# Products of two constants at ten stage boundaries of an fp32 two-block transformer kernel

## The chip, the core and the metric

The kernel runs on one core of a Trainium2 chip. A core has a matrix engine (TensorE, PE in the rows), a vector engine (VectorE, DVE), an activation engine (ScalarE, ACT), a general engine (GpSimd, POOL) and a queue that issues transfers (SyncE, SP). The engines run their own instruction streams and wait for each other on semaphores. The metric is device time in microseconds (us) of one execution, the median of several runs.

TensorE's clock has two levels, 2.4 GHz and 1.2 GHz. The trace records the granted clock as a share: 1.00 is 2.4 GHz, 0.50 is 1.2 GHz.

## What is computed

Two transformer blocks of two layers each, in fp32, over 256 tokens of width 1024. Cut to what matters here:

```python
def first_block(x, ...):
    for l in range(2):
        x = x + 0.5 * swiglu(rms_norm(x, ffn1_norm[l]), ffn1_w_gu[l], ffn1_w_down[l])
        x = x + hybrid_mixer(rms_norm(x, mix_norm[l]), w_in[l], ..., w_out[l])
        x = x + 0.5 * swiglu(rms_norm(x, ffn2_norm[l]), ffn2_w_gu[l], ffn2_w_down[l])
    return rms_norm(x, final_norm)

def second_block(x, ...):
    for l in range(2):
        h = hybrid_mixer_2(rmsnorm(x, pre_mix_norm[l]), ...)
        x = x + rmsnorm(h, post_mix_norm[l])
        h = conv_glu_ffn(rmsnorm(x, pre_ffn_norm[l]), ffn_up[l], ..., ffn_down[l])
        x = x + rmsnorm(h, post_ffn_norm[l])
    return x

def rms_norm(x, g):          # rmsnorm is the same
    return x * rsqrt(mean(x * x, -1) + 1e-6) * g
```

## The kernel before

Activations lie transposed: a tile holds 128 channels on the partitions and the 256 tokens along the free axis, so `x` is eight such chunks. All weights stream from HBM once, in slots of 1 MB (`raw`, two buffers). ScalarE rounds a slot to `w_hi`, VectorE computes the rest `w_lo` (L1517), and the ring of split slots is four deep. Activations are split in the same way (`xn`, `h`, `m`, `y`, `yb`, `ya`). Each fp32 product of the model is three products of the split parts, L514 to L516 in `mac`, and L519 to L521 in `mac_tok`, with 128x256 moving operands. `wide` computes two output tiles of 128 channels from a slot; `tokens` computes the transposed form; `down` contracts over the 22 chunks of `h`.

Block 1 runs, per layer, the stages `gu1`, `down1`, `in` (20 slots, attention and a gated spatial unit between them), `pb`, `pa`, `out`, `gu2`, `down2`. Block 2 runs, per layer, `qkv`, `side`, `out`, `gu`, `down`. Each engine has its own program with the stages in this order, and a hardware loop over the two layers of a block, so TensorE's program jumps back once in each block. Nothing schedules it but the order of the code and the semaphores.

A norm needs the sum of squares over all channels. ScalarE squares the eight chunks of `x` as they come out of the stage before, GpSimd adds them into `ssum` (L2049), and `mean_square` lets TensorE multiply `ssum` by the constant `ones_d`, which leaves the mean in every partition of PSUM bank 6 (`AUX`). ScalarE takes the root (`rms`, L1093) and VectorE the reciprocal (`rstd`, L1523). In block 1 the gains alone are applied before the next stage's products, and `rstd` is applied to their results. So those products need only the last chunks of `xn`, and `mean_square` runs between the first two output tiles of the stage. In block 2 some norms can't be put off: after `out`, `mean_square` (k = 1) is followed by `mean_square_direct`, which sums the squares `sq` of the new `x` in eight products (L535), and only then can `xn` be formed. After `down`, `mean_square` (k = 3) is followed by the norm, the addition to `x`, the squares of the next norm and the new `xn`. After block 1 the final norm is applied in the same way (`END1`).

The products in plain fp32 (L529, L535, L822 and others) are not split. `small_product` multiplies all of `xn` by a narrow matrix (`sm_hi` and `sm_lo`, 72 columns, in block 1's `in` after slot 1). `heads4` (L822) issues four products of 128x128 by 128x128.

Of the kernel before, what the change touches and what calls it, by code (L numbers as in the profile page):

```python
# [32 lines left out]
P = 128  # L33
# [104 lines left out]
def cycle(eng, count, period, body):  # L138

    groups = count // period  # L140
    if groups > 1:
        with eng.Fori(0, groups) as g:
            for j in range(period):
                body(j, g)
    else:
        groups = 0
    for j in range(groups * period, count):
        body(j, 0)


def layers(eng):
    return eng.Fori(0, DEPTH)


def program(nc, io, ctx):
# [6 lines left out]
    def fixed(name, shape):  # L162
        t = at_byte(name, shape, cursor[0])
        cursor[0] += (int(np.prod(shape)) * 4 + 31) // 32 * 32
        return t
# [11 lines left out]
    ones_d = fixed("ones_d", [P])  # L177
# [118 lines left out]
    ps = ctx.enter_context(nc.psum_tensor("ps", [P, 8, 512], F32))  # L296
    SC, AUX = 4, 6
# [153 lines left out]
    def run_of(at, k):  # L451

        return k - 1 if at[0] == 2 and k >= 2 else k
# [55 lines left out]
    def _(pe):  # L509
# [8 lines left out]
        def mac_tok(out, xh, xl, w, wl, first, last):  # L518
            pe.matmul(out, xh, w, start=first, stop=False)  # L519
            pe.matmul(out, xh, wl, start=False, stop=False)  # L520
            return pe.matmul(out, xl, w, start=False, stop=last)  # L521

        def mean_square(at, k, by_token=False):
            pe.wait_ge(summed.sem, summed.upto(at, 7 * run_of(at, k)))
            if by_token:
                for t in range(NT):
                    pe.matmul(ps[:, AUX, T + t:T + t + 1], ssum[:, t * P:(t + 1) * P], ones_d[:, 0:1],
                              start=True, stop=True)
            pe.matmul(ps[:, AUX, 0:T], ones_d[:], ssum[:], start=True, stop=True).then_inc(mean_sq.sem, 1)  # L529

        def mean_square_direct(at):

            for c in range(KC):
                pe.wait_ge(squared.sem, squared.upto(at, KC + c + 1))
                last = pe.matmul(ps[:, AUX, 0:T], ones_d[:], sq8[:, c], start=c == 0, stop=c == KC - 1)  # L535
            last.then_inc(mean_sq.sem, 1)

        def xn_ready(at, k, c):

            s = xn_lo_even if c % 2 == 0 else xn_lo_odd  # L540
            pe.wait_ge(s.sem, s.upto(at, k * KC // 2 + c // 2 + 1))

        def gate_up(at, st, k, prev):

            wide(at, st, 0, 0, xn, KC, k - 1, lambda: mean_square(at, k), prev)
            wide(at, st, 1, 0, xn, KC, None, None, prev)
            with pe.Fori(0, (FC - 2) // 4) as g:
                for j in range(2, 6):
                    wide(at, st, j, g, xn, KC)

        def slot(at, st, j, g=0):
            pe.wait_ge(lo.sem, lo.upto(at, st.slot0 + j + 4 * g + 1))
            r = (st.slot0 + j) % RING
            return w_hi[:, r], w_lo[:, r]

        def pair(at, st, i):

            if not isinstance(i, int) or i >= 2 or st.name != "in":
                pe.wait_ge(signals[st.free].sem, signals[st.free].upto(at, st.free0 + (i - 1) * st.free_by))
# [5 lines left out]
        def after(at, behind, q):  # L565

            signal, count, by = behind
            pe.wait_ge(signal.sem, signal.upto(at, count - by * (1 - q)))

        def behind(st):  # L570
            return signals[st.free], st.free0 + st.pairs * st.free_by, st.free_by

        def wide(at, st, j, g, x_of, chunks, k_norm=None, between=None, prev=None):

            whs, wls = slot(at, st, j, g)
            tiles = SLOT // P // chunks
            wh = whs.rearrange("p (c n) -> p c n", c=chunks)
            wl = wls.rearrange("p (c n) -> p c n", c=chunks)
            for f in range(tiles):
                q = (tiles // 2) * j + f // 2  # L580
                if f % 2 == 0 and prev is not None:
                    after(at, prev, q)
                elif f % 2 == 0:
                    pair(at, st, q + 4 * g)
                out = ps[:, 2 * (q % 2) + f % 2, 0:T]
                for c in range(chunks):
                    if k_norm is not None and f == 0 and j == 0:
                        xn_ready(at, k_norm, c)
                    last = mac(out, wh[:, c, f * P:(f + 1) * P], wl[:, c, f * P:(f + 1) * P],
                               x_of[:, c, 0], x_of[:, c, 1], c == 0, c == chunks - 1)  # L590
                last.then_inc(full.sem if f < tiles - 1 else used.sem, 1)
                if between and f == 0:
                    between()

        def down(at, st, hk):
            def tile(j, g):
                pair(at, st, j + 2 * g)
                out = ps[:, 2 * (j % 2), 0:T]
                for half in range(2):
                    pe.wait_ge(lo.sem, lo.upto(at, st.slot0 + 2 * j + half + 4 * g + 1))  # L600
                    pe.wait_ge(h_lo.sem, h_lo.upto(at, hk + (half + 1) * FC // 2))
                    r = (st.slot0 + 2 * j + half) % RING
                    wh = w_hi[:, r, 0:SLOT_DOWN].rearrange("p (c n) -> p c n", n=P)
                    wl = w_lo[:, r, 0:SLOT_DOWN].rearrange("p (c n) -> p c n", n=P)
                    for c in range(FC // 2):
                        k = half * FC // 2 + c
                        last = mac(out, wh[:, c], wl[:, c], h[:, k, 0], h[:, k, 1], k == 0, k == FC - 1)
                    last.then_inc(used.sem, 1)
            cycle(pe, st.pairs, 2, tile)
# [122 lines left out]
        with layers(pe) as layer:  # L732
            at = (1, layer)
            gate_up(at, st1["gu1"], 0, (x_new, 0, 1))
            stage_open(at, st1["gu1"])
            down(at, st1["down1"], 0)

            pe.wait_ge(ready.sem, 16 * N_TABLES)
            for k in range(20):
# [64 lines left out]
            pe.wait_ge(m_lo.sem, m_lo.upto(at, KC))  # L804
            for j in range(4):
                wide(at, st1["out"], j, 0, m, KC)
            gate_up(at, st1["gu2"], 2, behind(st1["out"]))
            stage_open(at, st1["gu2"])
            down(at, st1["down2"], FC)
        mean_square(END1, 0)  # L810
        with layers(pe) as layer:
            at = (2, layer)
            sq, ss, so = st2["qkv"], st2["side"], st2["out"]
# [196 lines left out]
            for b in range(2):  # L1010
                pe.matmul(ps[:, AUX + b, :], ones_q[:], q_diag[:, 2 * b:2 * b + 2].rearrange("p h q -> p (h q)"),
                          start=True, stop=False)
# [9 lines left out]
            pe.wait_ge(yb_lo.sem, yb_lo.upto(at, 2))  # L1022
            for j in range(4):
                wide(at, so, j, 0, y2, KC)
            mean_square(at, 1)
            mean_square_direct(at)
            cycle(pe, FC, 4, lambda j, g: wide(at, st2["gu"], j, g, xn, KC, 1))
            stage_open(at, st2["gu"])
            down(at, st2["down"], 0)
            mean_square(at, 3)  # L1030

    def slot_done(eng, at, st, j, g=0):

        eng.wait_ge(used.sem, used.upto(at, st.slot0 + j + 4 * g + 1))
# [1278 lines left out]
```

## Time and profile before

| | us |
|---|---|
| median of 3 runs | 2209.1 |
| lowest and highest run | 2204.98, 2214.56 |
| profiled execution, first to last instruction | 2211.2 |
| TensorE busy in it | 1995.0 (90%) |
| VectorE, ScalarE, GpSimd busy | 1243.9, 999.5, 703.1 |
| mean granted clock of TensorE | 0.945 |

The profiled execution's own time is its span of 2211.2 us. It lies 2.1 us above the median of the three runs and inside their range. A busy share says which engine is busiest; it doesn't say what an idle stretch waits for. That stands in the timeline, in brackets behind the instruction that ended the idle time: how long the engine sat, and whose result came last. "issue" in that place means that the engine waited for nothing that the profile shows.

### The profile page before, as it was taken

To read this page: it belongs to the slowest core of one execution; us is meant where nothing else is said; L and a number is where in the kernel's file an instruction comes from. 1 tells how busy PE (TensorE), PEld (TensorE's weight loads), DVE (VectorE), ACT (ScalarE), POOL (GpSimd) and SP (SyncE) were. 2 spreads that over 40 slices of the span, in tenths; PEclk is the share of its full clock that TensorE was granted. 3 is DMA by queue.
4 is the path that set the end of the run, shared out by engine and by line. 5 is a ranking of instruction groups with operands and counts; after the bars stand their busy time and mean duration, and the time that the engine had idled before them with its cause. 6 is when DMAs were issued, how large, how long until landed. Compare 5 with 4: busy or idle time off the path is not lost.

```text
span 2211.2 us, 42383 instructions
## 1 busy us (share of the span) xinstructions
PE 1995.0 (90%) x15702; PEld 1947.0 (88%) x15702; DVE 1243.9 (56%) x1541; ACT 999.5 (45%) x1323; POOL 703.1 (32%) x650
## 2 busy tenths in 40 slices
PE   5999988999999999888999888978999689869996
PEld 5999988999999999888999888967989689769996
DVE  4545575665456454765654565526664664356655
ACT  4434444544344344444443455444544363445443
POOL 3661211256317611211564123312331105122221
PEclk8999999999999998999999979988999789989998
DMA  5545433355455454333554522202445322124443
GB/s 184 190 149 192 160 115 134 136 188 190 150 181 202 153 174 173 115 134 119 186 190 148 186 85 96 96 27 107 171 153 170 115 96 96 39 77 152 162 159 135
DMA packets 52105, 314.37 MB, mean 142 GB/s; under 512 B 6928, under 2 KB 9744, under 8 KB 22928
## 3 DMA queue, kind: packets, MB, share of 16 engines
q1 hardware_dynamic: 48960, 311.09, 40.3%
q10 hardware_dynamic: 3024, 1.69, 0.3%
q8 instruction: 74, 1.21, 0.2%
q14 instruction: 47, 0.39, 0.1%
HBM read 311.70 MB, written 1.05 MB: 141 GB/s over the span
## 4 chain that ended last, share of the span: by engine, by line
PE 60%; issue 23%; DVE 5%; POOL 4%; ACT 4%; ACTq 1%; DMA 1%; DVEq 1%; SPq 0%; POOLq 0%
PE ps L514 18%; PE ps L515 18%; PE ps L516 18%; ACT w_hi L1067 2%; PE ps L519 1%; PE ps L521 1%; PE ps L520 1%; DVE conv L1835 1%; ACT conv L1111 1%; POOL lev_c L2149 1%; DMA raw<-in_in_dram 1%; POOL rope_tmp L2093 1%; POOL m L2130 1%; DVE v L2005 1%; DVE w_lo L1517 1%
## 5 line engine op out<-in xcount | busy, mean ns | idle before, releaser
L1517 DVE TENSOR_TENSOR w_lo<-raw,w_hi 128x2048 fp32r<-128x2048 f32 (+1 forms) x322 | 704.9, 2190 | 422.5 <-ACT w_hi L1067 420.8
L514 PE MATMUL ps<-xn,w_hi 128*128 128x256 f32 x2688 | 785.3, 292 | 74.3 <-DVE xn L1538 40.0
L515 PE MATMUL ps<-xn,w_hi 128*128 128x256 f32 x2688 | 773.8, 288 | 0.0
L516 PE MATMUL ps<-xn,w_lo 128*128 128x256 f32 x2688 | 772.9, 288 | 0.0
L1067 ACT ACTIVATE w_hi<-raw 128x2048 fp32r<-128x2048 f32 (+1 forms) x322 | 561.7, 1745 | 103.7 <-DMA raw<-in_down_dram 57.4
L514 PEld LDWEIGHTS ps<-xn,w_hi 128*128 128x128 f32 x2688 | 529.6, 197 | 87.2 <-DVE xn L1538 42.7
L515 PEld LDWEIGHTS ps<-xn,w_hi 128*128 128x128 f32 x2688 | 530.1, 197 | 0.6 <-issue 0.5
L516 PEld LDWEIGHTS ps<-xn,w_lo 128*128 128x128 f32 x2688 | 529.4, 197 | 0.0
L514 PE MATMUL ps<-h,w_hi 128*128 128x256 f32 x1056 | 301.2, 285 | 10.3 <-DVE conv L1835 5.6
L515 PE MATMUL ps<-h,w_hi 128*128 128x256 f32 x1056 | 300.0, 284 | 0.0
L516 PE MATMUL ps<-h,w_lo 128*128 128x256 f32 x1056 | 299.9, 284 | 0.0
L514 PEld LDWEIGHTS ps<-h,w_hi 128*128 128x128 f32 x1056 | 204.0, 193 | 11.6 <-issue 11.5
L2078 POOL TENSOR_TENSOR hv<-hv,rstd 128x256 f32<-128x256 f32 x88 | 156.3, 1776 | 169.9 <-DVE hv L1548 169.9
L515 PEld LDWEIGHTS ps<-h,w_hi 128*128 128x128 f32 x1056 | 204.1, 193 | 0.0
L516 PEld LDWEIGHTS ps<-h,w_lo 128*128 128x128 f32 x1056 | 204.0, 193 | 0.0
L2049 POOL TENSOR_TENSOR ssum<-ssum,sqb 128x256 f32<-128x256 f32 x98 | 91.3, 932 | 276.8 <-ACT sqb L1132 199.2
L1117 ACT ACTIVATE silu_gate<-silu_gate 128x256 f32<-128x256 f32 x88 | 36.8, 418 | 287.0 <-DVE silu_gate L1543 287.0
L2083 POOL TENSOR_TENSOR h<-hv,h 128x256 f32 (+1 forms) x132 | 157.8, 1196 | 23.5 <-POOL h L2081 22.5
L519 PE MATMUL ps<-w_hi,xn 128*128 128x256 f32 x512 | 152.2, 297 | 13.1 <-DVE w_lo L1517 13.1
L520 PE MATMUL ps<-w_lo,xn 128*128 128x256 f32 x512 | 148.1, 289 | 0.0
L521 PE MATMUL ps<-w_hi,xn 128*128 128x256 f32 x512 | 148.0, 289 | 0.0
L1548 DVE TENSOR_TENSOR hv<-silu_gate,ps 128x256 f32<-128x256 f32 x88 | 37.1, 421 | 153.4 <-PE ps L516 134.1
(300 smaller groups left out, 2724.3 us busy)
## 6 DMA issues: line engine op xcount, KB each, us to landing
raw<-in_gu_dram SPq DMA_DIRECT2D x132, 1024.0 KB, 4.7
raw<-in_in_dram SPq DMA_DIRECT2D x70, 1024.0 KB, 4.8
raw<-in_down_dram SPq DMA_DIRECT2D x96, 704.0 KB, 4.0
raw<-in_out_dram SPq DMA_DIRECT2D x16, 1024.0 KB, 4.9
raw<-in_pb_dram SPq DMA_DIRECT2D x4, 1024.0 KB, 4.8
raw<-in_pa_dram SPq DMA_DIRECT2D x4, 1024.0 KB, 4.9
rows<-in_rows_dram SPq DMA_DIRECT2D x2, 768.0 KB, 6.6
x<-in_x_dram SPq DMA_DIRECT2D x1, 1024.0 KB, 4.9
```

The source lines that it names most:

```text
L514: pe.matmul(out, w, xh, start=first, stop=False)
L515: pe.matmul(out, w, xl, start=False, stop=False)
L516: return pe.matmul(out, wl, xh, start=False, stop=last)
L519: pe.matmul(out, xh, w, start=first, stop=False)
L520: pe.matmul(out, xh, wl, start=False, stop=False)
L521: return pe.matmul(out, xl, w, start=False, stop=last)
L1067: return act.activation(out, src, ACT.Copy)
L1517: dve.tensor_tensor(w_lo[:, r, 0:elems], raw[:, k % RAW_RING, 0:elems], w_hi[:, r, 0:elems], ALU.subtract).then_inc(lo.sem, 1)
L1548: dve.tensor_tensor(hv[:, j % 2], silu_gate[:, j % 2], ps[:, 2 * (j % 2) + 1, 0:T], ALU.mult)\
L2049: pool.tensor_tensor(ssum[:], ssum[:], sqb[:, c % 2], ALU.add).then_inc(summed.sem, 1)
L2078: pool.tensor_tensor(hv[:, j % 2], hv[:, j % 2], rstd[:, 0:T], ALU.mult).then_inc(h_scaled.sem, 1)
L2083: pool.tensor_tensor(h[:, i, 1], hv[:, j % 2], h[:, i, 0], ALU.subtract).then_inc(h_lo.sem, 1)
```

## The change

A helper `idle_products(n)` issues `n` plain fp32 products of the constant 128x128 tile `ones_d` with itself into columns 384 to 511 of PSUM bank 7 (`AUX + 1`). Nothing reads them there, and they wait for nothing and signal nothing. It is called at these places on TensorE, and in no other engine's program:

| place | products | executed |
|---|---|---|
| block 1, between `down1` and `in` | 10 | in each of 2 layers |
| block 1, between `out` and `gu2` | 8 | in each of 2 layers |
| block 1, after `down2` (end of the layer loop's body) | 10 | in each of 2 layers |
| after `mean_square(END1, 0)` | 44 | once |
| block 2, between `out` and `mean_square` (k = 1) | 6 | in each of 2 layers |
| block 2, between it and `mean_square_direct` | 16 | in each of 2 layers |
| block 2, between that and `gu` | 16 | in each of 2 layers |
| block 2, between `down` and `mean_square` (k = 3) | 8 | in each of 2 layers |
| block 2, after it (end of the layer loop's body) | 56 | in each of 2 layers |

```diff
--- before.py
+++ after.py
@@ -520,6 +520,11 @@
             pe.matmul(out, xh, wl, start=False, stop=False)
             return pe.matmul(out, xl, w, start=False, stop=last)
 
+        def idle_products(n):
+
+            for _ in range(n):
+                pe.matmul(ps[:, AUX + 1, 3 * P:4 * P], ones_d[:], ones_d[:], start=True, stop=True)
+
         def mean_square(at, k, by_token=False):
             pe.wait_ge(summed.sem, summed.upto(at, 7 * run_of(at, k)))
             if by_token:
@@ -734,6 +739,7 @@
             gate_up(at, st1["gu1"], 0, (x_new, 0, 1))
             stage_open(at, st1["gu1"])
             down(at, st1["down1"], 0)
+            idle_products(10)
 
             pe.wait_ge(ready.sem, 16 * N_TABLES)
             for k in range(20):
@@ -804,10 +810,13 @@
             pe.wait_ge(m_lo.sem, m_lo.upto(at, KC))
             for j in range(4):
                 wide(at, st1["out"], j, 0, m, KC)
+            idle_products(8)
             gate_up(at, st1["gu2"], 2, behind(st1["out"]))
             stage_open(at, st1["gu2"])
             down(at, st1["down2"], FC)
+            idle_products(10)
         mean_square(END1, 0)
+        idle_products(44)
         with layers(pe) as layer:
             at = (2, layer)
             sq, ss, so = st2["qkv"], st2["side"], st2["out"]
@@ -1022,12 +1031,17 @@
             pe.wait_ge(yb_lo.sem, yb_lo.upto(at, 2))
             for j in range(4):
                 wide(at, so, j, 0, y2, KC)
+            idle_products(6)
             mean_square(at, 1)
+            idle_products(16)
             mean_square_direct(at)
+            idle_products(16)
             cycle(pe, FC, 4, lambda j, g: wide(at, st2["gu"], j, g, xn, KC, 1))
             stage_open(at, st2["gu"])
             down(at, st2["down"], 0)
+            idle_products(8)
             mean_square(at, 3)
+            idle_products(56)
 
     def slot_done(eng, at, st, j, g=0):
```

TensorE's program between block 2's `out` and the direct mean, before: the last products of `out`, the product of `ssum` (L529), and the first of the eight products of `sq` (L535).

```order
L514 MATMUL ps<-y_143,w_hi 128x256
L515 MATMUL ps<-y_143,w_hi 128x256
L516 MATMUL ps<-y_143,w_lo 128x256
L524 REGISTER_ALU
L529 MATMUL ps<-ssum,ones_d 128x256
L534 REGISTER_ALU
L535 MATMUL ps<-sq_141,ones_d 128x256
```

The same place in the changed kernel, where the lines are numbered 5 higher:

```order
L514 MATMUL ps<-y_143,w_hi 128x256
L515 MATMUL ps<-y_143,w_hi 128x256
L516 MATMUL ps<-y_143,w_lo 128x256
L526 MATMUL ps<-ones_d 128x128 x6
L529 REGISTER_ALU
L534 MATMUL ps<-ssum,ones_d 128x256
L526 MATMUL ps<-ones_d 128x128 x16
L539 REGISTER_ALU
L540 MATMUL ps<-sq_141,ones_d 128x256
```

Six products now stand ahead of the product of `ssum`, and sixteen between it and the first square; nothing has changed places.

TensorE's program at the end of block 1, before: the end of the loop in `down2` (L142), the end of the layer loop (L732) with its jump back to `gu1`, and `mean_square(END1, 0)`.

```order
L516 MATMUL ps<-h,w_lo 128x256
L142 REGISTER_ALU
L142 COMPARE_AND_BRANCH
L732 REGISTER_ALU
L732 COMPARE_AND_BRANCH
L529 MATMUL ps<-ssum,ones_d 128x256
L811 UNCONDITIONAL_BRANCH
```

And in the changed kernel, where the layer loop is L737:

```order
L516 MATMUL ps<-h,w_lo 128x256
L142 REGISTER_ALU
L142 COMPARE_AND_BRANCH
L526 MATMUL ps<-ones_d 128x128 x10
L737 REGISTER_ALU
L737 COMPARE_AND_BRANCH
L534 MATMUL ps<-ssum,ones_d 128x256
L526 MATMUL ps<-ones_d 128x128 x44
```

The ten products stand ahead of the layer loop's jump back, so TensorE's program reaches that jump behind them; the 44 stand ahead of block 2.

## Rows read from the trace of the kernel before

**Rows 1.** Timeline of TensorE, fp32 passes: start us, us, engine, line, operation, count.

```profile
1426.34 2.02 PE L822 MATMUL ps<-t_inv,lev_c 128*128 128x128 f32 x16
...
1442.38 1.27 PE L822 MATMUL ps<-v_new,k_dec 128*128 128x128 f32 x5
```

**Rows 2.** Stretches: length, busy per engine, then PEclk (granted clock), DMA share, GB/s.

```profile
242.40:252.60 10.20, 10.20 (x50) 10.20 (x50) 4.68 (x6) 2.33 (x3) 0.00 (x0) 0.50 0.45 176
...
853.40:870.40 17.00, 15.63 (x73) 15.63 (x74) 9.85 (x11) 3.91 (x6) 0.00 (x0) 0.50 0.34 124
...
1279.00:1283.40 4.40, 4.35 (x20) 4.35 (x21) 2.62 (x3) 1.26 (x5) 3.21 (x4) 0.50 0.01 4
...
1368.00:1437.00 69.00, 68.80 (x582) 66.92 (x581) 35.12 (x39) 28.57 (x43) 29.62 (x20) 1.00 0.26 92
...
1519.00:1525.80 6.80, 6.79 (x28) 6.13 (x28) 3.76 (x8) 4.94 (x8) 2.31 (x3) 0.50 0.01 2
...
1744.90:1751.00 6.10, 6.09 (x29) 6.10 (x29) 2.50 (x3) 1.71 (x7) 3.20 (x4) 0.50 0.01 4
```

**Rows 3.** Timelines, end of `down1` to `in`; brackets hold the idle time and its releaser.

```profile
224.80 0.28 PE L519 MATMUL ps<-w_hi,xn 128*128 128x256 f32 x1
...
235.62 1.92 ACT L1067 ACTIVATE w_hi<-raw 128x2048 fp32r<-128x2048 f32 x1 [0.83 <-DMA raw<-in_in_dram]
...
240.59 0.30 PE L519 MATMUL ps<-sm_hi,xn 128*128 128x72 f32 x1 [2.87 <-DVE sm_lo L1672]
...
854.77 0.43 PE L519 MATMUL ps<-sm_hi,xn 128*128 128x72 f32 x1 [4.33 <-DVE sm_lo L1672]
...
298.61 0.57 PE L519 MATMUL ps<-w_hi,xn 128*128 128x256 f32 x1 [6.53 <-DVE w_lo L1517]
...
915.31 0.57 PE L519 MATMUL ps<-w_hi,xn 128*128 128x256 f32 x1 [6.54 <-DVE w_lo L1517]
```

**Rows 4.** Timeline of TensorE, end of `out` to `gu2`, first layer.

```profile
450.27 0.28 PE L516 MATMUL ps<-m,w_lo 128*128 128x256 f32 x1
...
450.39 0.28 PE L514 MATMUL ps<-xn,w_hi 128*128 128x256 f32 x1
```

**Rows 5.** Timelines, end of `down2`: into the second layer, then into block 2.

```profile
645.43 0.38 PE L514 MATMUL ps<-xn,w_hi 128*128 128x256 f32 x1 [2.03 <-issue]
...
1265.35 0.70 PE L529 MATMUL ps<-ssum,ones_d 128*128 128x256 f32 x2 [2.97 <-POOL ssum L2049]
...
1279.05 0.58 PE L514 MATMUL ps<-xn,w_hi 128*128 128x256 f32 x1 [13.00 <-DVE xn L1538]
```

**Rows 6.** Timelines, end of block 2's `out` to `gu`, first layer.

```profile
1503.42 0.70 PE L529 MATMUL ps<-ssum,ones_d 128*128 128x256 f32 x2 [1.92 <-POOL ssum L2049]
...
1508.40 5.56 PE L535 MATMUL ps<-sq,ones_d 128*128 128x256 f32 x16 [4.28 <-ACT sq L1485]
...
1512.54 2.29 DVE L1517 TENSOR_TENSOR w_lo<-raw,w_hi 128x2048 fp32r<-128x2048 f32 x1
...
1514.74 1.75 DVE L1523 RECIPROCAL rstd<-rms 128x256 f32<-128x256 f32 x1
...
1518.41 0.39 PE L514 MATMUL ps<-xn,w_hi 128*128 128x256 f32 x1 [4.45 <-DVE xn L1538]
...
1523.74 0.58 PE L514 MATMUL ps<-xn,w_hi 128*128 128x256 f32 x1
```

**Rows 7.** Timelines, end of block 2's `down`: first layer, then the kernel's end.

```profile
1726.11 0.70 PE L529 MATMUL ps<-ssum,ones_d 128*128 128x256 f32 x2 [1.93 <-POOL ssum L2049]
...
1744.90 0.58 PE L514 MATMUL ps<-xn,w_hi 128*128 128x256 f32 x1 [18.10 <-DVE xn L1538]
...
2193.79 0.70 PE L529 MATMUL ps<-ssum,ones_d 128*128 128x256 f32 x2 [1.93 <-POOL ssum L2049]
...
2208.84 1.63 DVE L2001 TENSOR_SCALAR v<-x,gains 128x256 f32<-128x256 f32 x2
```

**Rows 8.** A stretch as in rows 2, around the end of `down2` in the first layer.

```profile
643.50:650.00 6.50, 4.57 (x36) 4.52 (x37) 3.01 (x3) 4.40 (x7) 1.43 (x2) 1.00 0.40 159
```

## Prediction

> **What bounds the kernel now.** I read four views: busy shares, TensorE's timeline, granted clock by stretch, and the bracket behind each instruction that ended an idle time. TensorE is busy for 90% of the span, so the span is its work at its pace plus its waits. Whatever is added to it where it doesn't wait is added to the span. In a full stage the products of the split parts start 0.12 us apart [rows 4]. At the lower clock, 50 of them took 10.20 us [rows 2]. So a restart at 1.2 GHz costs about half of the TensorE time that it lasts, where nothing else is late.
>
> For each of the ten places three questions are to be asked: does TensorE wait there, for whom, and at which clock does it go on?
>
> **The price of one product.** Plain fp32 products appear as two passes each: the eight products of `sq` in the code are the 16 records of L535 [rows 6]. Sixteen passes with a 128x128 moving tile took 2.02 us at the full clock. Less the last one's 0.28 us that is 0.116 us from start to start, so 0.23 us per product. At the lower clock five took 1.27 us [rows 1]: less 0.41 us for the last, 0.215 us a pass, 0.43 us a product. I take 0.23 us, since the clock was at 1.00 through 69 us in which many such passes ran [rows 2]. So 6, 8, 10, 16, 44 and 56 products take 1.4, 1.9, 2.3, 3.7, 10.2 and 13.0 us.
>
> The Trainium skill, "TensorE: Matmul & The Clock Gate", section "Back-to-back issue gap", gives N / 2.4 + 2.5 ns between isolated matmuls, which is 56 ns for 128 columns. By it ten products would take 0.6 us and all the terms below would shrink. The trace has twice that for each of two passes.
>
> **`out` to `gu2`, 8 products, twice.** TensorE doesn't wait here: the first product of `gu2` starts 0.12 us after the last of `out` [rows 4], and the clock is full. The products cover nothing, and the mean that the drain of `gu2` needs comes later by as much. Cost 2 x 1.9 = 3.7 us (1.86 each).
>
> **`down1` to `in`, 10 products, twice.** No wait either: the first product of `in` follows without a bracket [rows 3]. But two slots later TensorE waits 2.87 us (4.33 us in the second layer) for `sm_lo`. That comes from VectorE, behind a `w_lo` whose `w_hi` waited for a transfer [rows 3]. The transfer doesn't depend on the added products. So 2.3 us of delay disappears in this wait, at no cost; without that cover it would be 2 x 2.3. In return the wait shrinks by 2.3 us. TensorE now comes out of it at or into the lower clock, for 10.2 and 17.0 us [rows 2]. Part of this is the narrow product itself (72 columns), which stays. I expect the fall about 2.3 us later, so that 2.3 us more of the work runs at full pace: 1.1 us per layer, -2.2 in all. The bounds are 0 and half of both stretches' busy time, (10.2 + 15.6) / 2 = 12.9. That it reaches the end I read from the next long wait: it is 6.53 us in one layer and 6.54 in the other [rows 3], although the stretches ahead differ by 7 us, so that chain moves with TensorE.
>
> **After `down2`, 10 products, twice.** In the first layer the wait is 2.03 us and its releaser is "issue" [rows 5]: not data, and at the same stage end elsewhere (`down1`) TensorE didn't wait at all. What differs is the layer loop's jump back. Ten products ahead of the jump move it, and the 2.03 us come again behind them. So +2.3 us. If the 2.03 us were a wait for data it would be +0.1. The clock is full before and after [rows 8], so nothing comes back. In the second layer no jump is taken; TensorE waits 2.97 us for `ssum` [rows 5] and 2.3 fit: 0.
>
> **44 products after the final norm's mean.** 10.2 us in a wait of 13.00 us [rows 5]: they end some 2.8 us before `xn` comes. After 2.87 us of waiting the clock also fell at 240.59 [rows 2, 3]. I take 0; the bound is half of 4.35 us, -2.2 [rows 2].
>
> **Block 2, `out` to `gu`, 6 + 16 + 16, twice.** 1.4 us in 1.92, 3.7 in 4.28, 3.7 in 4.45 us [rows 6]: all covered, with under 1 us left each time. So the clock should stay full here. The eight products of `sq` then end earlier, but `rstd` starts at 1514.74 when the 2.29 us of `w_lo` on VectorE are over [rows 6]: that gain is 0. In the first tile of `gu` the chunks of `xn` come one by one; the eighth starts at 1523.74 [rows 6], and only from there to 1525.8, where the clock was full again [rows 2], does pace count. 2.1 us at half pace are 1.0 at full, less what the first pass still waits: -0.9 us per layer, -1.8 in all. Bounds: 0 and -3.4 each.
>
> **Block 2, `down` to the next layer, 8 + 56, twice.** 1.9 us in 1.93 [rows 7] doesn't delay the mean. 13.0 us in 18.10 leave 5 us idle before 1744.90, more than the waits after which the clock fell; the restart stays slow. The jump back, now behind the products, has those 5 us. 0, bound -3.0. At the kernel's end the 56 products stand behind the last mean (2193.79, 0.70 us) and end near 2207.5; VectorE works on `x` until 2210.5 [rows 7]. 0, and 7 us more if they ran at the lower clock.
>
> **Sum.** 3.7 + 2.3 - 2.2 - 1.8 = +2.0 us, on 2211.2 us. The median of the runs is 2.1 us lower, so 2209.1 + 2.0 = 2211.1 us.
>
> **Rivals.**
> - *The clock comes back everywhere.* All restarts run at 2.4 GHz, because it is enough that products ran in most of the wait. The stretches of rows 2 give (10.2 + 15.6 + 4.4 + 6.1) / 2 and twice 6.8 / 2: 24.9 us; less the 6.0 of pure cost that is -18.9, 2190 us. Against it: 2.8 and 5 us idle remain, and the narrow product stays. Half of it is needed to pass 0.5%. Chance 0.08. The Trainium skill, same page, section "What's actually happening", puts the ramp penalty under 1% of a typical span, 22 us here; the stretches' 24.9 us come out just above it.
> - *Nothing comes back.* The clock falls as before, since where it falls depends on where the waits lie. Then only 3.7 + 2.3 = 6.0 us stand: 2215.1 us. For it: each stage meets a changed timing, and falls elsewhere may grow. Chance 0.22.
> - *The jump back is hidden.* If the sequencer gets to the jump well before the products have run, +2.3 becomes +0.1: 2208.9 us. Chance 0.12.
> - *The products run at the lower clock.* That is the slower end, one mechanism: TensorE falls to 1.2 GHz on products that the clock's control doesn't count, and each takes 0.43 us. Then 8 cost 3.4 us twice, the jump's 10 cost 4.3, `down1`'s exceed 2.87 by 1.4, the second 10 their wait by 1.2, 44 (18.9 us) theirs by 5.9, block 2's 6 + 16 + 16 by about 5 per layer, 8 by 1.3 twice, 56 (24.1 us) by 5.8, and at the end by 7. Together 45 us, 2254 us. It decides from 0.27 us per product on (16 of them then fill 4.28 us), and passes 0.5% at about 0.33. Against it: rows 1 and the 1.00 of 1368 to 1437 [rows 2]. Chance 0.08.
>
> **Chances and range.** The forecast has 0.50. Forecast, nothing back and hidden jump together have 0.84, all within 0.5% (11 us, about what a measurement can tell from no change). Faster takes the first rival, 0.08; slower the last, 0.08; the same 0.84. The range takes the three inner cases, the bound of the `down1` term partly, and runs that spread over 10 us: 2202 to 2221.
>
> **What the new profile would show.** Two passes of L526 per product, 0.115 us apart. The first product of `gu2` 1.9 us behind the last of `out`. The wait for `sm_lo` near 0.6 and 2.0 us. At the jump, 2 us of "issue" behind the ten products. Clock 1.00 from the end of block 2's `out` to `gu`, `rstd` still behind `w_lo`. 0.50 at the restarts after 44 and 56. I am wrong if the restarts after 44 and 56 are at 1.00, if passes start over 0.15 us apart, or if the time of a stage between the places has changed by more than 3 us.

## The result, and the profile after

The changed kernel takes 2215.9 us, the median of 20 runs (2209.79 to 2222.04), beside 2208.19 us (2204.63 to 2215.04) for the kernel before in 20 runs on the same chip. The ratio is 1.0030 with a 95% interval of 1.0022 to 1.0038: 6.6 us slower, between 4.9 and 8.4 (the two medians lie 7.7 us apart; all differences below are the ratio's). Forecast were 2.0 us more. That is within the 0.5% that I called "the same", but more than three times the forecast.

First the page of the changed kernel: busy time, share and instructions of each engine, and the granted clock in 40 slices.

```profile
PE 2059.3 (93%) x16310; PEld 2009.6 (91%) x16310; DVE 1243.8 (56%) x1541; ACT 1000.0 (45%) x1323; POOL 701.7 (32%) x650
...
PEclk8999899999999999999999989989999989999999
```

TensorE is busy for 2059.3 us where it was 1995.0. The mean granted clock rose from 0.945 to 0.960, and the span rose too, from 2211.2 to 2215.2 us. So the products do raise the clock, and it buys no time.

**Where time was added.** Timeline of TensorE in the changed kernel, the end of `out` and then the end of `down2` in the first layer of block 1 (answering rows 4 and 5; the number in a bracket is the idle time ahead). The VectorE row is the making of the first weight tile of `gu1`.

```profile
451.30 1.95 PE L526 MATMUL ps<-ones_d 128*128 128x128 f32 x16
453.00 0.36 PE L514 MATMUL ps<-xn,w_hi 128*128 128x256 f32 x1
...
641.53 2.29 DVE L1531 TENSOR_TENSOR w_lo<-raw,w_hi 128x2048 fp32r<-128x2048 f32 x1 [2.15 <-ACT w_hi L1081]
...
645.07 2.39 PE L526 MATMUL ps<-ones_d 128*128 128x128 f32 x20
651.48 0.38 PE L514 MATMUL ps<-xn,w_hi 128*128 128x256 f32 x1 [4.02 <-DVE w_lo L1531]
```

The first is as forecast: 16 passes, and `gu2` starts behind them. The second isn't. Ten products take 2.39 us, but the idle time behind them is 4.02 us where it was 2.03 [rows 5]. From the start of the products to the first product of `gu1` are 6.41 us; before, the same stretch (from 0.12 us after the start of `down2`'s last product, where a next product would start) had 2.2 us. The bracket names `w_lo`, since a later one ended just before; but the first tile of `gu1` was ready at 641.53 + 2.29 = 643.82, 7.7 us before. What TensorE waits for there is what the experiments are about. Right behind it the clock falls, which it didn't before [rows 8]. That fall isn't the jump's alone: four kernels below that have no products at this place (the 10 after `down1` alone, block 2's alone, all but the 10, and the longer fillings) show it too, and in them `gu1` takes 130.0 to 130.1 us from its first product to the first of `down1`, as here; in the kernel before it takes 128.5.

**Where the clock changed.** Stretches of the changed kernel, with the columns of rows 2: `in`, both layers; behind the jump; the restart after the 44 products; block 2's `out` to `gu`; the restart after the 56; and the 44 and the 56 products themselves.

```profile
239.80:253.40 13.60, 12.97 (x61) 12.97 (x62) 6.46 (x7) 3.17 (x6) 0.00 (x0) 0.50 0.43 155
864.40:871.20 6.80, 6.80 (x34) 6.80 (x34) 4.90 (x6) 2.33 (x3) 0.00 (x0) 0.50 0.46 154
652.80:656.20 3.40, 3.40 (x18) 3.31 (x17) 0.00 (x0) 0.00 (x0) 0.00 (x0) 0.50 0.70 282
1280.90:1284.20 3.30, 3.30 (x16) 3.14 (x16) 2.17 (x3) 0.81 (x4) 2.76 (x4) 0.50 0.00 0
1485.70:1660.00 174.30, 166.75 (x1317) 159.20 (x1315) 117.68 (x148) 85.67 (x119) 50.72 (x73) 1.00 0.41 144
1748.50:1751.80 3.30, 2.75 (x13) 2.75 (x14) 2.92 (x4) 2.26 (x9) 2.89 (x4) 0.50 0.02 5
1267.50:1277.30 9.80, 9.80 (x88) 9.61 (x87) 9.43 (x15) 2.98 (x7) 3.57 (x4) 1.00 0.33 109
1730.00:1743.00 13.00, 13.00 (x114) 12.89 (x114) 11.92 (x20) 3.33 (x8) 3.40 (x4) 1.00 0.24 83
```

The last two are long stretches at full clock in which only the added products run. In the kernel before, the clock was at 0.50 in the same two waits (same columns):

```profile
1266.50:1279.00 12.50, 0.00 (x0) 0.00 (x0) 12.01 (x20) 4.68 (x14) 6.41 (x8) 0.50 0.24 84
1727.30:1744.80 17.50, 0.00 (x0) 0.00 (x0) 15.61 (x27) 4.30 (x12) 6.03 (x8) 0.50 0.19 62
```

TensorE's busy time there is 0.00. A low clock on an idle engine costs nothing, and a high one gives nothing back. A third wait of this kind is behind TensorE's last product, at the kernel's end. Most of the rise of the mean is this: by the clock's records the time at 0.50 fell from 247 to 179 us, and the part of it in which TensorE worked on the model's own products from 168 to 154.5 us only.

**The waits that the products fill.** Timeline of the changed kernel: `in`; then into block 2; then block 2's `out` to `gu`; then `down` to the next layer (answering rows 3 and 5 to 7).

```profile
240.43 0.43 PE L519 MATMUL ps<-sm_hi,xn 128*128 128x72 f32 x1 [3.02 <-DVE sm_lo L1686]
...
1267.31 9.99 PE L526 MATMUL ps<-ones_d 128*128 128x128 f32 x88
1280.51 0.38 PE L514 MATMUL ps<-xn,w_hi 128*128 128x256 f32 x1 [3.21 <-DVE xn L1552]
...
1507.57 0.70 PE L534 MATMUL ps<-ssum,ones_d 128*128 128x256 f32 x2 [0.58 <-POOL ssum L2063]
...
1512.55 5.52 PE L540 MATMUL ps<-sq,ones_d 128*128 128x256 f32 x16 [0.71 <-ACT sq L1499]
...
1516.68 2.28 DVE L1531 TENSOR_TENSOR w_lo<-raw,w_hi 128x2048 fp32r<-128x2048 f32 x1
1518.89 1.74 DVE L1537 RECIPROCAL rstd<-rms 128x256 f32<-128x256 f32 x1
...
1522.55 0.39 PE L514 MATMUL ps<-xn,w_hi 128*128 128x256 f32 x1 [0.92 <-DVE xn L1552]
...
1730.46 12.67 PE L526 MATMUL ps<-ones_d 128*128 128x128 f32 x112
1749.05 0.58 PE L514 MATMUL ps<-xn,w_hi 128*128 128x256 f32 x1 [5.92 <-DVE xn L1552]
```

Waits of 13.00, 1.92, 4.28, 4.45 and 18.10 us have become 3.21, 0.58, 0.71, 0.92 and 5.92. Waiting was replaced by products; nothing starts earlier for it. `rstd` still follows `w_lo` on VectorE (1516.68 + 2.28 = 1518.96).

### The profile page after: what moved, and what is told of

It reads as the page before. It is cut to its first block, busy times and chain, and to the rows that moved or that the text cites. A ratio compares the mean times of both kernels' runs of the same rounds, so it can differ in the third digit from the quotient of the medians.

```text
span 2215.2 us, 43599 instructions
## 1 busy us (share of the span) xinstructions
PE 2059.3 (93%) x16310; PEld 2009.6 (91%) x16310; DVE 1243.8 (56%) x1541; ACT 1000.0 (45%) x1323; POOL 701.7 (32%) x650
## 3 DMA queue, kind: packets, MB, share of 16 engines
HBM read 311.70 MB, written 1.05 MB: 141 GB/s over the span
## 4 chain that ended last, share of the span: by engine, by line
PE 60%; issue 24%; POOL 5%; DVE 4%; ACT 4%; ACTq 1%; DMA 1%; DVEq 1%; SPq 0%; POOLq 0%
PE ps L514 18%; PE ps L515 18%; PE ps L516 18%; DVE conv L1849 1%; PE ps L519 1%; PE ps L521 1%; PE ps L520 1%; ACT w_hi L1081 1%; ACT conv L1125 1%; POOL lev_c L2163 1%; DMA raw<-in_in_dram 1%; POOL rope_tmp L2107 1%; POOL m L2144 1%; DVE w_lo L1531 0%; ACTq L1217 0%
## 5 line engine op out<-in xcount | busy, mean ns | idle before, releaser
L514 PE MATMUL ps<-xn,w_hi 128*128 128x256 f32 x2688 | 783.1, 291 | 46.1 <-DVE w_lo L1531 18.9
L2097 POOL TENSOR_TENSOR h<-hv,h 128x256 f32 (+1 forms) x132 | 152.0, 1152 | 23.5 <-POOL h L2095 22.5
```

Of the source, the lines that this page charges most:

```text
L514: pe.matmul(out, w, xh, start=first, stop=False)
L2097: pool.tensor_tensor(h[:, i, 1], hv[:, j % 2], h[:, i, 0], ALU.subtract).then_inc(h_lo.sem, 1)
```

## The experiments

All kernels are the one before with some of the products (the helper `idle_products` is in each). A diff with only + lines is against the kernel before, one with - lines against the changed kernel. Every figure for a kernel is from 12 runs of it (11 for the 10 after `down1` alone and for two products) and 23 or 34 of the kernel before on the same chip. Differences in us are the ratio times some 2209 us. Each timeline is one execution. First the ten places in groups.

**The 10 after `down2` alone.**

```
             down(at, st1["down2"], FC)
+            idle_products(10)
         mean_square(END1, 0)
```

> Only the ten products after down2 of block 1 (run in both layers), nothing else of the change. Theory after the result: nearly the whole loss sits at the layer loop's jump back. The trace of the changed kernel shows 4.02 us of idle behind the ten products where before there were 2.03 us, and the clock falling behind it. So 2.3 (products) + 2.0 (longer idle) + 1.2 (restart at the lower clock) = about 5.5 us slower, ratio 1.0025, with about 4 us of idle behind the products. Rival, the prediction's price: the idle of 2.03 us comes again unchanged and the clock stays full, +2.3 us, ratio 1.001. Second rival: the 4.02 us were chance of one execution; then the idle here is about 2 us.

Measured: 1.0019 (1.0008 to 1.0030), 4.2 us more (1.8 to 6.6). One fifteenth of the products makes more than half of the 6.6 us, by the middle of the intervals. Timeline of this kernel at the jump:

```profile
643.17 2.39 PE L526 MATMUL ps<-ones_d 128*128 128x128 f32 x20
...
649.01 0.57 PE L514 MATMUL ps<-xn,w_hi 128*128 128x256 f32 x1 [3.44 <-issue]
```

Here the bracket says "issue", as in the kernel before: 3.44 us where 2.03 stood.

**All of the change but these 10.**

```
             down(at, st1["down2"], FC)
-            idle_products(10)
```

> The whole change without the ten products after down2. Theory: the jump's place is the loss, so this returns about 5.5 of the measured 6.6 us: within 2 us of the kernel before, ratio 0.9995 to 1.0010, idle at the jump 2.0 us. Rival: the loss is spread over all places (products ahead of gu2, ahead of in, restarts met by other clock falls); then this stays 4 us or more slower, ratio 1.002 or more.

Measured: 0.9993 (0.9980 to 1.0005), -1.5 us (-4.4 to +1.1). Without this call the change is level with the kernel before, although the products of all other places are left, the 8 after `out` too. The mean clock of its trace is 0.959, as in the full change. So most of the time lies at the jump. How much, this pair doesn't fix: taken out of the whole change the 10 give back 8.1 us, alone they cost 4.2, each with about 3 us to either side.

**The 8 after `out` alone.**

```
                 wide(at, st1["out"], j, 0, m, KC)
+            idle_products(8)
             gate_up(at, st1["gu2"], 2, behind(st1["out"]))
```

> Only the eight products between out and gu2, twice. Prediction's price: nothing covers them, 2 x 1.86 = +3.7 us, ratio 1.0017. Rival from the trace of the changed kernel: 0.69 us of each are taken by the wait of 0.24 us for the first drain of gu2 and the late start behind it, so +1.2 each, +2.3 us, ratio 1.0010.

Measured: 1.0016 (1.0001 to 1.0032), 3.5 us (0.2 to 7.1). The trace has `gu2` 1.7 us later at its start, and less behind its first slots, one of which TensorE enters in the kernel before after a wait of 0.24 us for `hv`, and in this one without: at the first product of `down2` 0.9 us are left (130.2 us from the end of `out` instead of 129.3), 1.8 in all for both layers, inside the interval. The kernels with these 8 among others have the same 0.9 in their traces. The kernel without the 10 measured -1.5 (-4.4 to +1.1) with them; with 1.8 us of cost here, its other places would have given back at least 0.7 us. A restart at the full clock in its trace (see the longer fillings) may be a part of that.

**Block 2's products alone** (44, and 6 + 16 + 16 + 8 + 56 in each layer).

```
         mean_square(END1, 0)
+        idle_products(44)
...
+            idle_products(6)
             mean_square(at, 1)
+            idle_products(16)
             mean_square_direct(at)
+            idle_products(16)
...
+            idle_products(8)
             mean_square(at, 3)
+            idle_products(56)
```

> Only the products behind block 1: 44 after the final norm's mean, and 6, 16, 16, 8 and 56 in block 2's layers. Prediction's price: 0 for 44, 8 and 56, and -0.9 us per layer from the first tile of gu, together -1.8 us, ratio 0.9992. Rival A: they give nothing, ratio 1.0000, because the pace of the first tile is set by xn and the clock falls elsewhere. Rival B: they cost, since each layer's stages meet other clock falls, over +1 us. Clock 1.00 from the end of out to the body of gu, 0.50 at the restart behind the 44 and the 56.

Measured: 1.0001 (0.9988 to 1.0014), +0.2 us (-2.7 to +3.1), with the mean granted clock at 0.961 instead of 0.945. This is the cleanest sight of the point above: the clock's mean rises by 0.016, and no change of the time shows.

**The 10 after `down1` alone.**

```
             down(at, st1["down1"], 0)
+            idle_products(10)
```

> Only the ten products between down1 and in, twice. Prediction's price: the 2.3 us vanish in the wait for sm_lo, and the clock falls 2.3 us later: -1.1 each, -2.2 us, ratio 0.9990. Rival: the wait absorbs them and nothing comes back, since the narrow product behind it lets the clock fall anyway: 0, ratio 1.0000. Rival: not absorbed, +4.6 us, ratio 1.0021. The wait for sm_lo itself should be 0.6 to 2.0 us long.

Measured: 0.9998 (0.9985 to 1.0011), -0.4 us (-3.3 to +2.4). The 2.3 us twice are absorbed in the wait for `sm_lo`: without that cover they would cost 4.6 us, which the interval excludes. The clock still falls, in this trace for 3.41 and 10.24 us where it was 10.24 and 17.07. But the second figure is no sign of the products: with none at this place, the trace of the 10 behind the jump (next) has 10.24 us there too. The forecast's -2.2 us is neither shown nor excluded.

**What happens at the jump.** Four explanations were open for the 4 us: (a) the start of a layer's code takes a time of its own after the jump, hidden in part under what is still queued; (b) straight-line code got longer; (c) it doesn't matter where the products stand, and the longer idle time was chance; (d) something that the load of the code collides with. First, the same ten products behind the jump:

```
             at = (1, layer)
+            idle_products(10)
             gate_up(at, st1["gu1"], 0, (x_new, 0, 1))
```

> Ten products at the top of block 1's layer loop, so behind its jump back instead of ahead of it, and nothing else of the change. In layer 0 they run before any data is there and cost nothing. Theory (the products ahead of the jump delay the jump itself, and the refetch behind it takes the same time again): here the idle in front of the products is that of before, 2.0 us, and then 2.3 us of products, +2.3 us at most, less what is waited for anyway; total idle around the jump 2.0 us. Rival (it is only the products' own 2.3 us, wherever they stand, and the longer idle of d2_only was chance): the same time as d2_only, which measured +4.2 us.

Measured: 1.0008 (0.9994 to 1.0022), 1.8 us (-1.3 to +4.8). In the timeline the idle time is ahead of the products and short, and `gu1` follows them at once:

```profile
642.82 2.47 PE L526 MATMUL ps<-ones_d 128*128 128x128 f32 x20 [1.52 <-issue]
645.04 0.36 PE L514 MATMUL ps<-xn,w_hi 128*128 128x256 f32 x1
```

From the end of `down2` to `gu1` are 3.9 us, against 5.8 with the products ahead of the jump and 2.2 with none. Ten products cost 1.7 us here, less than they last, and 3.6 there, so (c) falls by the timelines. The measured times, 1.8 and 4.2, have intervals that overlap and don't tell the two apart by themselves.

**Twice as many ahead of the jump.**

```
             down(at, st1["down2"], FC)
+            idle_products(20)
```

> Twenty products after down2 of block 1 instead of ten, nothing else of the change. Theory (idle behind the products is the fetch after a late jump, 3.4 to 4.0 us at ten): 4.6 us of products and 2 to 4 us idle behind them in layer 0; in the second layer 4.6 us of products in the 3.1 us until ssum is there, +1.5. Sum 4.6 + 0 to 2 + 1.5 = 6 to 8 us slower. If the time until the jump's data arrive counted from the last product of down2, the idle would shrink to about 0 to 1 us and the sum to about 4 us.

Measured: 1.0024 (1.0012 to 1.0036), 5.3 us (2.7 to 8.0), while ten more products last 2.2 us by themselves. The second layer's 20 outlast their wait of 2.97 us, but in the trace `xn` comes no later for it: block 2 starts 16.8 us after the end of `down2`, as in the kernel before. The first product of `gu1` comes 6.6 us after `down2`, against 5.8 with ten:

```profile
641.12 4.62 PE L526 MATMUL ps<-ones_d 128*128 128x128 f32 x40
...
647.72 0.38 PE L514 MATMUL ps<-xn,w_hi 128*128 128x256 f32 x1 [1.98 <-DVE w_lo L1523]
```

So the extra time at the jump is no fixed sum behind the products. With 20 the idle time is 1.98 us again, with 10 it was 3.44.

**The ten products as a loop of five times two**, which makes the code shorter by eight of them and adds jumps of its own:

```
             down(at, st1["down2"], FC)
+            with pe.Fori(0, 5):
+                idle_products(2)
```

> The ten products after down2 of block 1 as a hardware loop of five passes over two products, nothing else of the change: the same 2.3 us of TensorE's time ahead of the layer loop's jump back, but two products of code instead of ten. Theory (ten products of straight code make TensorE load a further piece of its program, and the load behind the jump waits for that one): without that piece the idle behind the products is that of before, 1.5 to 2.1 us, and the total from the last product of down2 to the first of gu1 4.0 to 4.4 us instead of 5.8; about +2.5 us, ratio 1.0011. Rival (the idle is longer because of the products' time ahead of the jump, not their code): 3.4 to 4.0 us idle behind them and +4.2 us, as d2_only.

Measured: 1.0021 (1.0010 to 1.0031), 4.6 us (2.2 to 6.9), with 3.49 us of idle time behind them. Code length, (b), falls: in the traces with 10 and 20 in a row a further piece of the program is loaded 0.4 and 0.6 us before the end of `down2`, in the loop's none, and both with ten wait alike.

```profile
647.24 2.39 PE L526 MATMUL ps<-ones_d 128*128 128x128 f32 x20
...
653.12 0.57 PE L514 MATMUL ps<-xn,w_hi 128*128 128x256 f32 x1 [3.49 <-issue]
```

**Two and six products.** If something collides, the cost should come in a step; if each product adds its share, it should not.

```
             down(at, st1["down2"], FC)
+            idle_products(2)
```

> Two products after down2 of block 1, nothing else of the change. Theory, from all traces so far: behind the layer loop's jump back TensorE loads a 16 KB piece of its program. The load starts 1.0 us behind the jump, but not while a weight transfer of 1 MB is under way: with the jump 1.8 us ahead of the end of down2 it starts before the next transfer (kernel before and six others, first product of gu1 1.9 to 2.3 us behind the end of down2); with ten products the jump comes into the transfer and the load starts when that ends (5.8 to 6.4 us). Two products move the jump by 0.46 us, the load would start 0.4 us ahead of the end of down2, the transfer 0.2 us ahead: still in front. So gu1 starts 2.3 to 2.8 us behind the end of down2, and the time is that of the kernel before, ratio 1.0002. Rival (each product adds its share of what ten cost, 0.38 us): 2.9 us; there the two hardly differ, this run is the lower half of a pair.

Measured: 0.9994 (0.9984 to 1.0004), -1.3 us (-3.5 to +0.9).

```
             down(at, st1["down2"], FC)
+            idle_products(6)
```

> Six products after down2 of block 1, nothing else of the change. Theory as for two: six products move the jump by 1.4 us, so the load would start 0.5 us behind the end of down2, inside the transfer, and waits for its end. So gu1 starts 5.8 to 6.4 us behind the end of down2, as with ten, with 4.4 to 5 us idle behind the products, and the time is that of d2_only: about +4 us, ratio 1.0018. Rival (each product adds its share of what ten cost, 0.38 us): 4.3 to 4.5 us, with 2.9 to 3.1 us idle, +2.3 us. Second rival (products and nothing else): 3.5 us, 2.1 us idle, +1.4 us.

Measured: 1.0019 (1.0009 to 1.0030), 4.2 us (2.0 to 6.6): as much as ten. Two products show no cost, six cost all of it. The timelines of the two kernels, one after the other:

```profile
641.26 0.60 PE L526 MATMUL ps<-ones_d 128*128 128x128 f32 x4
...
643.89 0.38 PE L514 MATMUL ps<-xn,w_hi 128*128 128x256 f32 x1 [2.03 <-issue]
```

```profile
644.91 1.50 PE L526 MATMUL ps<-ones_d 128*128 128x128 f32 x12
...
650.77 0.58 PE L514 MATMUL ps<-xn,w_hi 128*128 128x256 f32 x1 [4.36 <-issue]
```

What differs is in the DMA view, which lists the queues with packets, MB and share of the 16 engines. Kernel before, 641.3 to 643.2 us; the first line is that stretch in 40 slices:

```profile
DMA  0000000000000000000000900000000000009900
...
q1 hardware_dynamic: 7, 0.06, 23.6%
q8 instruction: 1, 0.02, 3.9%
```

The packet of the queue "instruction" at 642.4, 16 KB, I take for a piece of TensorE's program: the view doesn't name the engine, but in the table below it follows TensorE's jump. It comes ahead of the weight transfer (q1), which begins at the right edge. Now the kernel with six products, 644.3 to 648 us, and then 648 to 649:

```profile
DMA  0000096900049509894998999299299699949900
...
q1 hardware_dynamic: 137, 1.05, 79.7%
```

```profile
DMA  9800000000000000000000000000000000000000
...
q8 instruction: 1, 0.02, 6.0%
```

The weight transfer of 1.05 MB has begun first, and the program's piece comes when it is nearly over. `gu1` starts 2.8 us later. The instants, in us from the end of `down2`, taken 0.12 us after its last product starts (the jump is the start of the sequencer's branch instruction in the trace, the piece the start of the first 16 KB packet behind it):

| products ahead of the jump | jump | program's piece | first product of `gu1` | idle behind products | ratio |
|---|---|---|---|---|---|
| none (before) | -1.8 | -0.9 | +2.2 | 2.03 | 1 |
| 2 | -1.6 | -0.1 | +2.6 | 2.03 | 0.9994 |
| 6 | -0.6 | +3.1 | +5.9 | 4.36 | 1.0019 |
| 10 | +0.35 | +3.0 | +5.8 | 3.44 | 1.0019 |
| 10, as a loop | +0.6 | +3.1 | +5.9 | 3.49 | 1.0021 |
| 10, whole change | +0.3 | +3.6 | +6.4 | 4.02 | 1.0030 |
| 20 | +2.6 | +3.6 | +6.6 | 1.98 | 1.0024 |
| 10 behind the jump | -1.8 | -0.8 | +3.9 (products +1.7) | none (1.52 ahead) | 1.0008 |

In all of them `gu1` (or, in the last row, the products) starts 2.5 to 3.1 us after the piece of program. The piece comes 0.9 to 1.4 us after the jump if no weight transfer is in its way, and else up to 0.45 us before the end of the transfer's last packet, some 3 us after `down2`, wherever in the transfer the jump falls. So between 2 and 6 products there is a step of 3.2 us in the start of `gu1`, and then none until the jump itself comes as late as the transfer's end. SP's issue of that transfer isn't moved by the products (642.07 us in the kernel before, 642.01 with ten). (d) stands, and (a) holds as a part of it.

The same order holds elsewhere in the kernel. By the packet records, the trace of the kernel before has 192 single weight transfers of 1.05 MB, some 3.5 us each and 30% of the span. Of its 74 pieces on this queue 20 start inside one of these, all in the last fifth. Over the 14 kept traces 306 pieces start inside such a transfer, 275 of them in the last fifth; if they came at any time alike it would be some 61. The 31 others say that it isn't a strict rule.

What this doesn't show is why the load seldom passes the transfer; it was seen as an order in time only. The transfer wasn't moved or made shorter, which would have been the direct test.

**Longer fillings in block 2.** With block 1's calls gone, I fitted the counts so that less idle time is left at the restarts:

```
         mean_square(END1, 0)
-        idle_products(44)
+        idle_products(54)
...
             mean_square(at, 3)
-            idle_products(56)
+            idle_products(68)
```

> Block 2's products alone, with 54 instead of 44 after the final norm's mean and 68 instead of 56 at the end of the layers, so that under 1 and about 3 us stay idle before the restarts; no products in block 1. If a restart at the full clock is worth half of its former time at the lower one (4.4 and 6.1 us), this is 2.2 + 3.0 us faster than block2_only, which measured the same as before: ratio 0.9977, clock 1.00 at both restarts. Rival: the clock fall only moves to a later stretch or xn arrives no earlier, so nothing is gained: ratio 1.0000.

Measured: 0.9994 (0.9982 to 1.0007), -1.3 us (-4.0 to +1.5). Timeline of TensorE at the two restarts:

```profile
1279.17 0.39 PE L514 MATMUL ps<-xn,w_hi 128*128 128x256 f32 x1 [0.98 <-DVE xn L1549]
...
1744.55 0.39 PE L514 MATMUL ps<-xn,w_hi 128*128 128x256 f32 x1 [3.12 <-DVE xn L1549]
```

After 0.98 us of idle time the clock stayed at 1.00, after 3.12 it was at 0.50 within a microsecond. What one kept restart is worth (2.2 us at most by rows 2) is below what the runs tell apart, but the traces show it. In the kernel before, 38.0 us pass from the end of `down2` until block 2 has its first 96 weight products and the narrow products behind them done and goes on. Here it is 37.9, and the clock falls again at 1294.8, within that stretch. In the trace of all but the 10, 44 products began at the lower clock, took 11.25 us and left 1.57 us idle; the clock then stayed at 1.00 until 1298.6, and the same stretch took 36.6 us. So the kept restart gave 0.1 us once and 1.4 us once.

**All gains and no cost, as far as they were known then**: the 10 after `down1`, block 2 with 56 and 73, nothing after `out` and `down2`.

```
-            idle_products(8)
             gate_up(at, st1["gu2"], 2, behind(st1["out"]))
             stage_open(at, st1["gu2"])
             down(at, st1["down2"], FC)
-            idle_products(10)
         mean_square(END1, 0)
-        idle_products(44)
+        idle_products(56)
...
-            idle_products(56)
+            idle_products(73)
```

> A version meant to beat both kernels: ten products between down1 and in, block 2's 6, 16, 16 and 8, 56 after the final norm's mean and 73 at the end of block 2's layers; none between out and gu2 and none after down2 of block 1. Theory: -0.5 us from the first (d1_only measured 0.9998) and up to -2 us from the restarts (tuned measured 0.9994): ratio 0.9985 to 0.9995, idle of about 0.6 us before the restart of block 2 and about 2 us before that of its second layer, the clock 1.00 at both. Rival: nothing is gained anywhere, since clock falls move elsewhere: ratio 1.0000.

Measured: 1.0001 (0.9986 to 1.0015), +0.2 us (-3.1 to +3.3). A miss. The timeline shows two ways in which fitted counts fail:

```profile
1265.78 14.99 PE L526 MATMUL ps<-ones_d 128*128 128x128 f32 x112
1280.52 0.36 PE L514 MATMUL ps<-xn,w_hi 128*128 128x256 f32 x1
...
1727.08 16.46 PE L526 MATMUL ps<-ones_d 128*128 128x128 f32 x146
1745.89 0.38 PE L514 MATMUL ps<-xn,w_hi 128*128 128x256 f32 x1 [2.35 <-DVE xn L1550]
...
1748.43 0.34 PE L514 MATMUL ps<-xn,w_hi 128*128 128x256 f32 x1 [1.92 <-POOL xn L2065]
```

56 products take 14.99 us here instead of 12.67, since the wait ahead of them let the clock fall; no wait is left behind them, so they ran into the start of block 2. Block 2 starts 18.9 us behind `down2` instead of 16.8, but at the full clock it makes up for that: the stretch of 38.0 us is 36.9 here, 1.1 us of gain. And behind 73 the restart meets two waits, so that the clock fell all the same; there the same stretch behind `down` has 44.3 us instead of 42.0, 2.3 us of loss. No kernel of this study is measurably faster than the one before.

## Why the prediction was right, and where it was not

- **After `down2`: the step that failed.** The prediction has "the 2.03 us come again behind them. So +2.3 us". That the products move the jump was right (the rival in which the jump is hidden, 2208.9 us, is out: 1.0019 for this place alone). That the 2.03 us are a fixed time behind it was wrong. They are the rest of a load that starts about 1 us after the jump, and the load meets the weight transfer as soon as the jump is later by an amount between 0.25 us (2 products) and 1.2 us (6). The trace of the changed kernel has 6.4 us where 2.2 stood, +4.2; this place alone has +3.6 in its trace and measured +4.2 (1.8 to 6.6), not 2.3. The fall of the clock behind it comes on top in these two traces (`gu1` takes 1.6 and 2.8 us more than before), but one of 1.5 us is also in four traces without the products, so it isn't counted here. Rows 5 and 8 already held a hint that I passed over: the first row has "issue" as its releaser, and the second has DMA at 0.40 in that same stretch.
- **`out` to `gu2`.** Forecast +3.7, measured +3.5 (0.2 to 7.1). The agreement is partly luck: the traces have +1.7 us a layer at the start of `gu2` and only 0.9 at its end, 1.8 in all. "The products cover nothing" was wrong by that half.
- **`down1` to `in`.** That the products cost nothing holds. Forecast were waits near 0.6 and 2.0 us; in the trace they are 3.02 us in the first layer and too short for a bracket in the second, since `sm_lo` itself comes at another time in each execution: in the ten traces without products there the wait is 1.7 to 4.3 us long. The -2.2 us are not confirmed: -0.4 (-3.3 to +2.4).
- **Block 2, 6 + 16 + 16.** The forecast's picture holds in each point: idle times of 0.58, 0.71 and 0.92 us, clock 1.00 through 1485.7 to 1660 us, `rstd` behind `w_lo`. Its -1.8 us are not to be seen in the time: block 2 alone measured +0.2 (-2.7 to +3.1). Nor are they in the traces: from the first product of `out` to the first of `down` a layer took 182.4 to 183.6 us in the nine kernels without these products, and 182.4 to 183.1 in the five with them.
- **44, 8, 56 and the kernel's end.** As forecast: clock 0.50 at both restarts, nothing gained, nothing lost. But at the first one that isn't certain with 44: in the trace of all but the 10 it was at 1.00. At the end the last 56 products run 12.67 us from 2198.32, to 2210.99, and VectorE finishes later:

```profile
2198.32 12.67 PE L526 MATMUL ps<-ones_d 128*128 128x128 f32 x112
...
2212.85 1.63 DVE L2015 TENSOR_SCALAR v<-x,gains 128x256 f32<-128x256 f32 x2
```

- **The products' price.** 2.39 us for ten, 9.99 for 44 and 12.67 for 56; forecast were 2.3, 10.2 and 13.0. The gap that the Trainium skill's section "Back-to-back issue gap" ("TensorE: Matmul & The Clock Gate") gives for isolated matmuls, 56 ns for 128 columns, is not that of these plain fp32 products: the trace has two passes of 112 ns.
- **The rivals.** "Nothing comes back" (2215.1) is the nearest, 6.0 us against 6.6 measured, and its claim that no time comes back agrees with the times of all parts. Its sum is right by luck, though: it is 3.7 + 2.3, where the traces have 1.8 after `out` and 4.2 at the jump. And the clock did come back, for the most part in stretches without work. "Clock comes back everywhere" falls by the restarts at 0.50, "products at lower clock" by the passes of 0.112 us (its 45 us are some 2 too low by its own terms, which changes nothing).

The parts measured alone give 4.2 + 3.5 + 0.2 - 0.4 = 7.5 us against 6.6 for the whole; their intervals are each about 3 us to either side, so the sum is no closer than that. The forecast's -4.0 us of gains from the clock are the larger part of the miss: the parts that should have brought them measured -0.4 and +0.2. Whether some of it exists stays open; it is within 3.3 us of nothing at both places. So the time fell into the forecast's range, but its terms were off to both sides: the jump too low by 1.9 us, `out` too high by 1.9 in the traces, and 4.0 us of gains that no run shows.

## What to carry to other kernels

Before work is put ahead of a loop's jump back, look in the DMA view for the engine's program being loaded and for what the queues carry 1 to 4 us later: work that moves the jump into a large transfer can cost the rest of that transfer, and it costs it in a step. The same work behind the jump cost 1.7 us in the timeline, no more than it lasts. A rise of the mean granted clock is no gain by itself: weigh each stretch at the lower clock by TensorE's busy time in it, and count it only where nothing else ends the wait that follows. All of this is read from one kernel.

## What the runs showed that I had not expected

- TensorE's sequencer reaches the jump 1.8 us before the last product ahead of it ends, and TensorE goes on 3.5 to 4.2 us after the jump even with no transfer in the way. So about 1.8 us of such a restart are hidden, and 2.03 us are seen as "issue".
- A program load of 16 KB came behind a weight transfer of 1.05 MB that had begun before it: 2.5 to 3.7 us from jump to load instead of 0.9 to 1.4. In 14 traces 275 of the 306 loads that start inside such a transfer do so in its last fifth.
- Plain fp32 products of constants held the clock at 1.00 through stretches of 9.8 and 13 us. The first idle time of 3.21 us after them let it fall again; those of 0.98 and 1.57 us didn't.
